# Routing stage of a two-block transformer kernel: the gate row moved from the projection's output to its weights, the residual added from PSUM by halves, and the tiles of the projection in another order

## What is computed

```python
x = _layernorm(ALPHA * x + g1 * (mixed[:, CTX_LEN:] @ w_out[l]), ln1_g[l], ln1_b[l])
ffn = _hier_moe(_modulate(x, sh2, sc2), rt_g[l], rt_g_b[l], rt_e[l], rt_e_b[l], ex_gate[l], ex_up[l], ex_down[l])
x = _layernorm(ALPHA * x + g2 * ffn, ln2_g[l], ln2_b[l])
```

## Time and profile before

| | |
|---|---|
| median of 3 runs | 3051.98 us |
| lowest, highest | 3046.80, 3055.32 us |
| span of the profiled execution | 3053.0 us |
| TensorE busy in it | 2849.0 us (93%) |
| VectorE busy | 1833.1 us (60%) |
| ScalarE busy | 1272.0 us (42%) |
| GpSimd busy | 789.1 us (26%) |
| routing stage, from its first load to the last tile's tokens | 2318.7 to 2401.2 us of the span |

### The profile page before, as it was taken

How to read it: one execution, slowest core, us unless ns; L and a number is a source line. 1 busy time by engine, 2 the same in 40 slices (tenths; PEclk the granted TensorE clock), 3 DMA queues, 4 the chain that set the end, 5 groups by cost and what they waited for, 6 DMA issues and landing times. The chain is left out here.

```text
span 3053.0 us, 54461 instructions
## 1 busy us (share of the span) xinstructions
PE 2849.0 (93%) x22525; PEld 2301.8 (75%) x22525; DVE 1833.1 (60%) x2580; ACT 1272.0 (42%) x1628; POOL 789.1 (26%) x427
## 2 busy tenths in 40 slices
PE   9889999999999998999999989878989699999994
PEld 7467888889777777888868877567885478888883
DVE  3766663120343445666246977676755789988997
ACT  3544232232333334232234322423332277777775
POOL 2013444434332312444420000010000124544431
PEclk9999999999999999999999999889999799999997
DMA  4633422232211112222222200241003489999996
GB/s 171 235 138 110 97 96 97 97 135 90 83 67 59 70 56 83 98 96 96 96 97 111 69 23 12 87 155 45 32 17 122 159 321 365 369 369 361 368 364 259
DMA packets 83394, 440.91 MB, mean 144 GB/s; under 512 B 19712, under 2 KB 22784, under 8 KB 34816
## 3 DMA queue, kind: packets, MB, share of 16 engines
q1 hardware_dynamic: 73920, 429.63, 38.6%
q0 software_dynamic: 9280, 8.43, 0.8%
HBM read 423.30 MB, written 37.77 MB: 151 GB/s over the span
## 5 line engine op out<-in xcount | busy, mean ns | idle before, releaser
L85 POOL TENSOR_TENSOR ring_lo<-ring,unit_hi 128x2048 fp32r<-128x2048 f32 x110 | 507.2, 4611 | 1046.5 <-ACT unit_hi L74 1046.5
L146 PE MATMUL wide<-h_hi,unit_hi 128*128 128x512 f32 x1296 | 516.5, 399 | 13.8 <-DVE h_lo L566 5.0
L148 PE MATMUL wide<-h_hi,ring_lo 128*128 128x512 f32 x1296 | 507.9, 392 | 0.0
L147 PE MATMUL wide<-h_lo,unit_hi 128*128 128x512 f32 x1296 | 507.6, 392 | 0.0
L3399 DVE TENSOR_TENSOR ex_w_lo<-ring,ex_w_hi 128x2048 fp32r<-128x2048 f32 x194 | 441.7, 2287 | 45.6 <-ACT ex_w_hi L3394 44.0
L3394 ACT CAST ex_w_hi<-ring 128x2048 fp32r<-128x2048 f32 x194 | 369.5, 1907 | 114.3 <-DMA ring<-in_weights 105.6
L74 ACT CAST unit_hi<-ring 128x2048 fp32r<-128x2048 f32 x114 | 217.7, 1909 | 389.9 <-PE wide L148 384.6
L146 PEld LDWEIGHTS wide<-h_hi,unit_hi 128*128 128x128 f32 x1296 | 245.0, 189 | 74.1 <-issue 15.4
L148 PEld LDWEIGHTS wide<-h_hi,ring_lo 128*128 128x128 f32 x1296 | 244.9, 189 | 52.7
L147 PEld LDWEIGHTS wide<-h_lo,unit_hi 128*128 128x128 f32 x1296 | 245.3, 189 | 49.4 <-issue 0.2
L391 DVE TENSOR_TENSOR ffn_hidden_lo<-ffn_whole,ffn_hidden_hi 128x512 f32 (+1 forms) x44 | 201.3, 4576 | 51.0 <-ACT ffn_hidden_hi L366 51.0
(11 more groups left out here) (573 smaller groups left out, 5684.8 us busy)
## 6 DMA issues: line engine op xcount, KB each, us to landing
ring<-in_weights SPq DMA_DIRECT2D x356, 1024.0 KB, 6.5
rw_F<-factors SPq DMA_DIRECT2D x9, 1024.0 KB, 5.1
factors<-rp_out SPq DMA_DIRECT2D x4, 1280.0 KB, 5.3
factors<-rp_out SPq DMA_DIRECT2D x4, 1024.0 KB, 5.1
ex_both<-pair_rows_out SPq DMA_DIRECT2D x4, 1024.0 KB, 8.1
x<-in_x SPq DMA_DIRECT2D x8, 256.0 KB, 6.3
x_kept<-x SPq DMA_DIRECT2D x1, 2048.0 KB, 12.2
x<-x_kept SPq DMA_DIRECT2D x1, 2048.0 KB
```

The lines of the kernel that those rows point to most:

```text
L85: pool.tensor_tensor(self.lo[n % RING][:, :], self.ring[n % RING][:, :], self.hi[n % 2][:, :].bitcast(F32), ALU.subtract).then_inc(self.lo ...
L146: pe.matmul(dst, a[0], b[0], start=start, stop=False)
L147: pe.matmul(dst, a[0], b[1], start=False, stop=False)
L148: return pe.matmul(dst, a[1], b[0], start=False, stop=stop)
```

## The change

The gate row is now applied to the weights: GpSimd multiplies each chunk's 128 x 1024 of the projection's weights, in place in the ring, by the gate row, eight products in all, and TensorE waits for them chunk by chunk. SyncE loads the gate row directly behind weight unit 0. VectorE no longer multiplies by the gate; it adds each half of the projection from PSUM straight to the residual and takes that half's statistics before the next half's sum. TensorE multiplies tile 0 to its end before it goes on with tile 1, interleaves the transposes of x in another way, and does tile 3 in two passes, one for each half, each of which VectorE can take by itself. ScalarE's list is the same.

```diff
+    def part(self, dve, i, src):
+        self.step(dve.bn_stats(self.parts[:, i, :], src), i == 1)
...
             def _(sp):
-                for n in range(2):
-                    w.load(sp, w.at + n)
+                w.load(sp, w.at)
+                sp.dma_start(rows.gate, gate_of).then_inc(gate_loaded, 16)
+                w.load(sp, w.at + 1)
                 sp.dma_start(x[:, :, :], kept).then_inc(head.x_back, 16)
...
             def _(pool):
+                experts.begin(pool)
+                pool.wait_ge(gate_loaded, 16)
+                for k in range(DC):
+                    unit = w.arrived(pool, 0, k // 2)
+                    of = unit[:, k % 2 * D:(k % 2 + 1) * D]
+                    pool.tensor_tensor(of, of, rows.gate, ALU.mult).then_inc(weights_gated, 1)
                 experts.gpsimd(pool)
...
-                        unit = w.arrived(pe, 0, k // 2)
+                        pe.wait_ge(weights_gated, k + 1)
+                        unit = w.ring[(w.at + k // 2) % RING]
...
-                        if t == TT - 1 and k % 2 == 1:
+                        if t == TT - 1 and halves[-1] == 1 and k % 2 == 1:
                             mm.then_inc(w.used, 1)
...
                 head.tensor_squares(pe)
-                tile(0, (0, 1), 0, MC)
+                for n in range(2):
+                    tile(0, (0, 1), n, n + 1)
+                    tile(1, (0, 1), n, n + 1)
                 head.tensor_spread(pe, 0)
                 head.tensor_spread(pe, 1)
-                for n in range(MC):
-                    tile(1, (0, 1), n, n + 1)
-                    if n < 2:
-                        head.tensor_spread(pe, 2 + n)
-                    else:
-                        turn_x(0, n - 2)
+                for n in range(2, MC):
+                    tile(0, (0, 1), n, n + 1)
+                    head.tensor_spread(pe, n)
+                turn_x(0, 0)
+                tile(0, (0, 1), MC, MC + 2)
+                turn_x(0, 1)
+                tile(0, (0, 1), MC + 2, DC).then_inc(tile_done, 1)
                 for n in range(2):
-                    tile(2, (0,), 2 * n, 2 * n + 2)
                     turn_x(1, n)
-                for t in range(2):
-                    for n in range(2):
-                        tile(t, (0, 1), MC + 2 * n, MC + 2 * n + 1)
-                        turn_x(2 + t, n)
-                        last = tile(t, (0, 1), MC + 2 * n + 1, MC + 2 * n + 2)
-                    last.then_inc(tile_done, 1)
-                tile(2, (0,), MC, DC)
+                    last = tile(1, (0, 1), 2 + 3 * n, 5 + 3 * n)
+                last.then_inc(tile_done, 1)
+                for n in range(4):
+                    turn_x(2 + n // 2, n % 2)
+                    tile(2, (0,), 2 * n, 2 * n + 2)
...
-                tile(3, (0, 1), 0, DC)
+                tile(3, (0,), 0, DC).then_inc(tile_done, 1)
+                tile(3, (1,), 0, DC)
...
                     for half in range(2):
                         cols = slice(half * T, (half + 1) * T)
-                        dve.tensor_tensor(h[:, t, cols], c.bank[2 * t + half], rows.gate[:, cols], ALU.mult).then_inc(gated, 1)
-                    dve.wait_ge(gated, 2 * t + 2)
-                    dve.wait_ge(x_grown, 2 * t + 2)
-                    dve.tensor_tensor(normed[:, t, :], normed[:, t, :], h[:, t, :], ALU.add).then_inc(added, 1)
-                    dve.wait_ge(added, t + 1)
+                        if t == TT - 1 and half == 1:
+                            dve.wait_ge(w.used, w.at + U_OUT2)
+                        dve.wait_ge(x_grown, 2 * t + half + 1)
+                        dve.tensor_tensor(normed[:, t, cols], normed[:, t, cols], c.bank[2 * t + half], ALU.add).then_inc(added, 1)
+                        dve.wait_ge(added, 2 * t + half + 1)
+                        norm.part(dve, half, normed[:, t, cols])
```

More of the change, by code:

```diff
@@ L2914, in begin, with vector @@
         self.step(dve.memset(self.eps[:, :], LN_EPS))
-    def vector(self, dve, n, src, mid, dst, scale, shift):
-        for i in range(2):
-            self.step(dve.bn_stats(self.parts[:, i, :], src[:, i * T:(i + 1) * T]), i == 1)
+    def part(self, dve, i, src):
+        self.step(dve.bn_stats(self.parts[:, i, :], src), i == 1)
+    def vector(self, dve, n, src, mid, dst, scale, shift, whole=True):
+        for i in range(2 if whole else 0):
+            self.part(dve, i, src[:, i * T:(i + 1) * T])
         dve.bn_aggr(self.stats[:, n, :], self.parts[:, :, :].rearrange("p i s -> p (i s)")).then_inc(self.measured, 1)
@@ L2931, with route_stage @@
 NOBODY = 1 << 20
-def route_stage(nc, c, w, o, x, kept, g, bonus, rows, hT, consts, loads, route, tokens, tail_loads, tail_loaded, tail_rows, pair_rows, out, places):
+def route_stage(nc, c, w, o, x, kept, g, bonus, rows, gate_of, hT, consts, loads, route, tokens, tail_loads, tail_loaded, tail_rows, pair_rows, out, places):
     NR = E_GROUPS + EXPERTS
@@ L3029, in turn_h @@
                     if t < 2:
-                        pe.wait_ge(gated, 2 * (2 * t + 1))
+                        pe.wait_ge(added, 2 * (2 * t + 1))
                     else:
@@ L3041, in logits_of @@
                     if t == 0:
-                        pe.wait_ge(gated, 2 * 2)
+                        pe.wait_ge(added, 2 * 2)
                         pe.wait_ge(loaded, 16 * len(loads))
@@ L3108, in _ @@
                 for t in range(TT):
-                    if t < TT - 1:
-                        dve.wait_ge(tile_done, t + 1)
-                    else:
-                        dve.wait_ge(w.used, w.at + U_OUT2)
+                    dve.wait_ge(tile_done, t + 1)
                     for half in range(2):
                         cols = slice(half * T, (half + 1) * T)
-                        dve.tensor_tensor(h[:, t, cols], c.bank[2 * t + half], rows.gate[:, cols], ALU.mult).then_inc(gated, 1)
-                    dve.wait_ge(gated, 2 * t + 2)
-                    dve.wait_ge(x_grown, 2 * t + 2)
-                    dve.tensor_tensor(normed[:, t, :], normed[:, t, :], h[:, t, :], ALU.add).then_inc(added, 1)
-                    dve.wait_ge(added, t + 1)
-                    norm.vector(dve, 2 * t, normed[:, t, :], normed[:, t, :], normed[:, t, :], rows.scale1, rows.shift1).then_inc(normed_ready, 1)
+                        if t == TT - 1 and half == 1:
[4 more added lines that the diff above has]
+                        norm.part(dve, half, normed[:, t, cols])
+                    norm.vector(dve, 2 * t, normed[:, t, :], normed[:, t, :], normed[:, t, :], rows.scale1, rows.shift1, False).then_inc(normed_ready, 1)
                     dve.wait_ge(normed_ready, t + 1)
@@ L3419, in sync, with begin @@
         tail.sync(sp)
+    def begin(pool):
+        pool.memset(blank[:, :], 0.0).then_inc(blank_ready, 1)
     def gpsimd(pool):
-        pool.memset(blank[:, :], 0.0).then_inc(blank_ready, 1)
         pool.wait_ge(tokens_stored, 16 * TT)
@@ L3619, in experts_of @@
     e = Bag()
-    e.sync, e.gpsimd, e.tensor, e.scalar, e.vector = sync, gpsimd, tensor, scalar, vector
+    e.sync, e.begin, e.gpsimd, e.tensor, e.scalar, e.vector = sync, begin, gpsimd, tensor, scalar, vector
     e.hi, e.lo, e.rounds_ready, e.slots_ready = hi, lo, rounds_ready, slots_ready
@@ L3757, in second_block @@
             rows.gate, rows.scale1, rows.shift1, rows.scale2, rows.shift2 = [sm(f"row_{n}", [P, D])[:, :] for n in ("g1", "ln1_g", "ln1_b", "sc2", "sh2")]
-            loads = [(rows.gate, mod_rows[GATE1].partition_broadcast(P)), (rows.scale1, a["ln_rows"][0].partition_broadcast(P)),
+            loads = [(rows.scale1, a["ln_rows"][0].partition_broadcast(P)),
                      (rows.shift1, a["ln_rows"][1].partition_broadcast(P)), (rows.scale2, mod_rows[SCALE2].partition_broadcast(P)),
@@ L3761, in second_block @@
                      (iota[:, :], a["iota"]), (earlier[:, :], a["earlier"]), (pairs[:, :, :, :], a["pairs"])]
-            route_stage(nc, c, w, mixed, x, kept, r.g, r.bonus, rows, hT, (rt, rt_bias, iota, earlier, pairs), loads, route, tokens, tail_loads, tail_loaded, tail_rows, pair_rows, out, places)
+            route_stage(nc, c, w, mixed, x, kept, r.g, r.bonus, rows, mod_rows[GATE1].partition_broadcast(P), hT, (rt, rt_bias, iota, earlier, pairs), loads, route, tokens, tail_loads, tail_loaded, tail_rows, pair_rows, out, places)
 COLS = {}
```

6 lines of the change are left out of this document (3 added, 3 removed).

## The result

The changed kernel took 3064.19 us (median of 20 runs, 3051.94 to 3071.07); the kernel before, run beside it, 3054.09 us (20 runs, 3046.80 to 3069.56). The ratio is 1.0028, 95% interval 1.0019 to 1.0037, which is 8.6 us more (5.8 to 11.3); the two medians lie 10.1 us apart, within that interval. The profiled execution has a span of 3059.6 us, 6.6 above the one before, at the same mean granted clock (0.969). That this comes within 0.3 us of the 3059.9 forecast for it is chance: the execution is 1.8 us longer ahead of the routing stage, 8.8 longer in it, and 4.0 shorter behind it.

What follows compares the result with a forecast made beforehand. The prediction took routing's chain (TensorE's last transposes of x, ScalarE's root, VectorE's tiles) to bound the kernel. Order 3.4 + wait 2.0 - tiles 3.3 + contention 4.8 = +6.9 us, giving 3058.9 us, range 3051 to 3066.

Steps and rivals of the forecast that it cites:

- What bounds the stage: Routing: TensorE's last transposes of x, ScalarE's copy and root, then VectorE's tiles set the end, moving the total one for one.
- Order, +3.4: TensorE's new order puts 38 products instead of 34 ahead of the last transposes of x, 3.4 us later.
- Tiles, -3.3: VectorE's tiles shrink from 11.01 to 9.90 us; tiles 1 to 3 give back 3.3 us.
- tile 0's early end: TensorE ends tile 0 after 20 products instead of 28, 6.9 us sooner, hidden behind the later last transposes.
- The wait for gated weights, +2.0: At the projection's start TensorE waits for GpSimd's first product and so begins 2.0 us late.
- Contention, +4.8: GpSimd's products and VectorE's operations with two SBUF inputs take turns in the head norm, delaying tile 0's end by 4.8 us.
- The mis-sized step: In the projection, TensorE waits for tile 0's last chunk and ends tile 0 at 2353.4 us.
- No contention: Rival: GpSimd's products do not block VectorE's head norm; +2.1 us, 3054.1 us in all; chance 0.15.
- GpSimd not giving way: Rival: queued GpSimd products go ahead of VectorE's head norm, +9.0 us; chance 0.18, shared with dearer products.
- Faster without the late roots: Rival: the last transposes of x don't bind, TensorE's end of the projection does; -3.6 us, 3048.4 us; chance 0.05.
- The shift taken up by the loop: Rival: the weight stream in the experts' loop absorbs routing's delay, leaving 3052 us; chance 0.05.

Runs made afterwards that it cites:

- e1: Changed kernel with ScalarE taking the first three roots between its copies of x instead of after all eight; routing stage 85.70 us, ratio to before 0.9988.
- e4: Kernel before with only TensorE's order of the changed kernel; routing stage 85.90 us against 82.47 before, ratio 1.0024.
- e6: Kernel before with VectorE adding halves straight from PSUM and no gate product anywhere; routing stage 79.05 us against 82.47 before, ratio 0.9989.
- e2: Changed kernel without GpSimd's eight products, gate left out, TensorE waiting only for the weights' arrival; routing stage 82.51 us, ratio to before 0.9995.
- e9: Changed kernel with GpSimd only writing zeros to a spare tensor, TensorE waiting for these writes chunk by chunk; routing stage 86.52 us, ratio to before 1.0010.
- e3: Changed kernel with GpSimd's products written to a spare tensor and TensorE not waiting for them one by one; routing stage 91.43 us, ratio to before 1.0021.
- e8: Changed kernel with unread filler products keeping TensorE busy in its two waits; routing stage 89.68 us against 91.23, ratio to before 1.0021.
- e5: Changed kernel with three roots between ScalarE's copies, the gate product on VectorE by halves, nothing on GpSimd; routing stage 77.90 us, ratio to before 0.9983.

## Why the prediction was right, point by point

- **What bounds the stage** held. The last transposes, one ScalarE copy and one root, then VectorE's tiles: 2374.80, 2376.02, 2376.34, 9.88 us a tile. e1 showed the root's place in ScalarE's list to be the reason, by moving only that.
- **Order, +3.4**: e4 gave +3.43. **Tiles, -3.3**: e6 gave -3.42, and the changed kernel's tile was 9.88 us for 9.90. Together e2 gave +0.04 for +0.1. One reading in passing was short: tile 0's early end was put at 6.9 us, eight products; it was 8.6 (e4), since four groups of transposes of 0.44 us went behind it as well. Nothing in the sum hung on it.
- **The wait for gated weights, +2.0.** The gate row landed so that GpSimd began 6.71 us into the stage (5.97 was forecast), and its product took 2.35 us undisturbed (2.27 was forecast), so TensorE began the projection 9.12 us into the stage instead of 6.28 (2325.01), 2.8 us late. Taken alone (e9) the wait costs 4.0 us, because its matmuls are slow behind it. Contention alone costs 8.9 us (e3), and both together 8.7: the wait vanishes beside contention. The prediction's own times say so too. Its 4.8 us is the distance from TensorE's end of tile 0 with the wait (2348.6) to the end by VectorE's chain (2353.4), and that chain starts from GpSimd and not from TensorE. So 2.0 + 4.8 is one cost, that of contention, cut in two; read as two separate costs it would mislead.
- **Contention, +4.8**: VectorE's chain was right as put, turn by turn, one instruction each, with the reciprocal and L2877 untouched. From the stage's start the gain of chunk 1 ended at 28.43 us (28.07 forecast) and the fourth chunk was ready at 33.25 (32.87 forecast). The size, 91.23 - 86.52 = 4.7 us on top of the wait, agrees partly by luck: both ends came out 2 us later than forecast, the one with the wait alone (e9) mostly through slow matmuls behind the first wait, the one with both mostly through slow matmuls behind the second.
- **The mis-sized step is the one behind it**: TensorE "now waits for the last chunk of tile 0: it ends tile 0 at 2353.4", 34.7 us into the stage. The first sum came at 36.96, 2.3 later. TensorE didn't wait for the last chunk: from the fourth spread (2346.98) to tile 0's end its timeline shows no wait, and the chunk was ready 3.7 us ahead of the sum. By the prediction's own numbers this second path, spread, eight products and two groups of transposes behind VectorE's L2877 of chunk 1 (2343.9 + 0.7), ends at 2353.2 and so is as long as the one through the last chunk. It took 10.54 us where it took 9.08 at full clock (e8). A wait of 2.5 us on TensorE was priced at its length alone; its lower clock behind it cost 1.5 us more. VectorE's chain, 0.4 late, is half of the rest; the other 0.4 are gaps between one engine's end and the next one's start that the sum had too short. That carried through to the end, 91.23 for 89.4.
- **The rivals.** No contention: refuted by L2880 and L2883 at 2.1 to 2.7 us and by e3 against e2. GpSimd not giving way: refuted by the same rows, since VectorE got its turn behind each product. Faster without the late roots: not here, but e1 and e5 show it. The shift taken up by the loop: the twenty runs of each kernel put the time at 5.8 to 11.3 us more, which leaves room for a part of it and not for the whole.

## What to carry to other kernels

An engine that stands idle is not free: before moving an elementwise product to GpSimd, list what VectorE does in that stretch with two inputs in SBUF, and count for each of them what is left of the GpSimd instruction that is running (here 1.2 to 2.1 us each, with products of 2.35). Finishing a piece earlier on one engine is worth nothing until each later engine's list lets that piece through, so read those lists first; here three square roots moved up in ScalarE's list shortened the stage by 5.5 us. Costs on parallel chains are not to be added (4.0 and 8.9 us alone, 8.7 together): measure or work out each alone and both together. Where two chains come out level, look at what each leaves out.

## What the runs showed of the hardware

- **TensorE's clock was down behind waits of 2.2 to 2.8 us.** In the 4 us that hold the end of the first wait the granted clock was 0.69 (changed kernel, wait of 2.76 us) and 0.72 (e9, 2.24 us), partly at 1.2 and partly at 2.4 GHz, and sixteen matmuls of 512 columns took 8.63 to 8.83 us instead of 7.13. Spreads and transposes behind such a wait took about twice as long (2.05 for 1.02, 1.06 for 0.60). Where TensorE was kept busy (e8) it stayed at 1.00. I had not expected it: in the kernel before, the stretches from 2320 to 2332 us all stood at 1.00.
- **GpSimd and VectorE, both with queued work that reads SBUF, took strict turns.** GpSimd's product took 2.35 us at its shortest and 2.79 at the median of the eight; VectorE's operations of 0.69 us with two inputs in SBUF became 1.9 to 2.8 us long, one each between two products. The eight products lasted 21.18 us, of which 8 x 2.35 = 18.8 are their own.
- **GpSimd's writes alone cost VectorE nothing here**: 14.85 us of memsets in the same stretch changed the stage by 0.02 us.
